# A chunked RWKV-7 recurrence on one core: doubling products over the changed columns only, and next-unit operands made on GpSimd

## The chip, the cores and the metric

One NeuronCore of a Trainium2 chip runs the whole program. The metric is the device time of one execution in microseconds. The engines are TensorE (PE, with its weight loads shown apart as PEld), VectorE (DVE), ScalarE (ACT), GpSimd (POOL) and SyncE (SP, which issues DMAs).

## The reference

Two transformer-like layers on 512 tokens of width 1024. The first has neighbourhood attention beside a gated linear attention, and a convolutional FFN. The second has windowed attention beside a bidirectional RWKV-7 recurrence, a gated merge, an FFN and a per-layer embedding. The change is in the recurrence:

```python
def step(state, inp):                      # rwkv7_bidir_scan, both directions
    r_t, w_t, k_t, v_t, a_t, b_t = inp
    sa = einsum('dbhij,dbhj->dbhi', state, a_t)
    state = state * w_t[..., None, :] + sa[..., :, None] * b_t[..., None, :] + v_t[..., :, None] * k_t[..., None, :]
    y = einsum('dbhij,dbhj->dbhi', state, r_t)
# decay = exp(-exp(-softplus(-w_raw) - 0.5)), a = sigmoid(a0 + al @ a2), kk = k * k_k normalised per head
# k_dir = k * (1 + (a - 1) * k_a); the scan gets (r, decay, k_dir, v, -kk, kk * a)
```

There are 8 heads of 64 and two directions. All matrix work of this stage is fp32.

## The kernel before

The program is a sequence of blocks: mixer, FFN, attention, recurrence, merge and FFN. Every block writes its engine programs out by hand, with counted semaphores. No scheduler moves anything, and each engine works through its own list in order.

The recurrence block (`rwkv_block`) cuts the 512 tokens into 8 chunks of 64 and works in 8 **units**. Unit u is the pair of a head group `fi = u // 2` (two heads, so 128 features on the partitions) and a direction `d = u % 2`. For each unit it does four things.

- It makes the operands. ACT makes `sg` and `rate` by sigmoid (`rates`), DVE a running sum (`sums`: a scan, then one or two tensor operations), and ACT three exponentials (`decays`). DVE then makes `kdir` and a new `rate` (`directed`, three operations) and `bz`, `pc`, `a_s`, `b_s`, `k_s` and `r_s` (`scale`, six operations). PE transposes `a_s`, `b_s`, `k_s` and at times v (`turn`). `turn` and `attention` wait for four counts of `tt_done` per unit.
- It makes five sets of within-chunk products (`attention`, line 2013), which DVE masks.
- It inverts a triangular 64x64 matrix per chunk and head by **doubling** in five rounds, k = 1 to 5 (`double`). Each round is split by head `hh`. PE makes z = ab·x (8 matmuls, two records each), ACT copies z out of PSUM (line 2227), PE makes the products for x and x_t, and DVE writes those entries of x and x_t that the level's mask selects (`copy_predicated`, lines 2368 and 2370). The last round makes x_t alone. At level k only blocks of 2^k columns of one parity change, but all 64 columns are computed and copied.
- It makes the late products (`late`): w and u from x_t (`wr`, 128 columns per matmul), `turn` of the next unit, and then products for the state, the output and the transfer between chunks.

The side work of unit u+1 sits inside the rounds of unit u. On DVE its place is written out by hand:

```python
if k == 1 and u % 2: unit_keys(u // 2 + 1)
elif k == 2:         sums(u + 1)
elif k == 3:         directed(u + 1)
elif k == 4:         scale(u + 1)
```

On ACT, `rates(u + 1)` stands after k = 1 and `decays(u + 1)` after k = 3, each behind the two z copies of its round and each with a load of an activation table. GpSimd has no work in this block. SP loads `lora_g` at the end, behind all of `tt_done`.

After the eight units the block scans over the chunks, normalises and gates.

Of the kernel before, what the change touches and what calls it, by code (L numbers as in the profile page):

```python
# [1877 lines left out]
def rwkv_block(nc, io, C, PV, zr, rw_t):  # L1878
# [6 lines left out]
    with ExitStack() as ctx:  # L1885
# [6 lines left out]
        def column(name, k=0):  # L1892
# [32 lines left out]
                             "ka1_done", "gate_sig"))  # L1925
        levels_loaded, levels_done, masks_loaded, gate_loaded = (
            sem(n) for n in ("levels_loaded", "levels_done", "masks_loaded", "gate_loaded"))
        side_done, side_read, summed, c_done, e_done, kd1, kd_done, tt_done, bonus_done = (
# [8 lines left out]
                             "gstd", "grs", "yn", "yt", "scaled", "gl_done", "with_bonus", "rw_done"))  # L1937

        tiles = lambda a: a.rearrange("p (a b) -> p a b", a=NB)
        tile = lambda a, t: a[:, t * P:t * P + P]  # L1940
# [8 lines left out]
        hp = lambda hh: slice(64 * hh, 64 * hh + 64)  # L1949
        level = lambda side, k: four(levels[:, side, k, :])  # L1950
        R_, K_, V_ = 0, RW_FI, 2 * RW_FI
# [10 lines left out]
        @block.sync  # L1962
        def _(sp):
            sp.dma_start(lora[0:64], io["lora_w"].rearrange("d p n -> p d n")).then_inc(in_loaded, 16)
            sp.dma_start(lora[64:128], io["lora_a"].rearrange("d p n -> p d n")).then_inc(in_loaded, 16)
            at = len(CHUNK_MASKS) * CH
            sp.dma_start(level_in, io["levels"][:, at:]).then_inc(levels_loaded, 16)
            sp.dma_start(masks[:].rearrange("p a b -> p (a b)"), io["levels"][:, 0:at]).then_inc(masks_loaded, 16)
            sp.wait_ge(tt_done, 4 * NU)
            sp.dma_start(lora_g, io["lora_g"]).then_inc(gate_loaded, 16)  # L1970

        @block.tensor
        def _(pe):
# [23 lines left out]

            def attention(u):
                fi, d = unit(u)
                pe.wait_ge(tt_done, 4 * (u + 1))  # L2000
                kinds = ((b_s, a_s, 4, 0), (a_s, b_s, 2, 0), (k_s, r_s, 2, W), (b_s, r_s, 0, 0), (k_s, a_s, 0, W))
# [22 lines left out]
            def double(u, k):  # L2024

                for hh in range(2):
                    if k == 1:
                        pe.wait_ge(a_read, 5 * u + 2)
                    else:
                        pe.wait_ge(cp_done, pr_at(u, k - 1, hh, 1))  # L2030
                        pe.wait_ge(z_read, NZ * u + 2 * (k - 2) + hh + 1)
                    block_products(lambda half, t: bank[hp(half), 4 + hh, t * CH:t * CH + CH],
                                   lambda half, t: ab_t[hp(half), hh, t, :], lambda half, t: x[hp(half), hh, t, :]).then_inc(z_done, 1)
                for hh in range(2):
                    pe.wait_ge(z_read, NZ * u + 2 * (k - 1) + hh + 1)
                    if k < LEVELS - 1:
                        if k == 1:
                            pe.wait_ge(a_read, 5 * u + 3)
                        block_products(lambda half, t: bank[hp(half), 2 + hh, t * CH:t * CH + CH],
                                       lambda half, t: x_t[hp(half), hh, t, :], lambda half, t: z[hp(half), hh, t, :]).then_inc(pr_done, 1)  # L2040
                    if k == 1:
                        pe.wait_ge(a_read, 5 * (u + 1))
                    block_products(lambda half, t: bank[hp(half), hh, t * CH:t * CH + CH],
                                   lambda half, t: z[hp(half), hh, t, :], lambda half, t: x_t[hp(half), hh, t, :]).then_inc(pr_done, 1)

# [113 lines left out]
        def _(act):  # L2159
            def rates(u):  # L2160

                fi, d = unit(u)
                if u:
                    act.wait_ge(tt_done, 4 * u)
                act.wait_ge(side_done, SIDE * u + 1)
# [51 lines left out]
            for u in range(NU):  # L2217
# [33 lines left out]
        def _(dve):  # L2251
            def sums(u):
# [14 lines left out]

            def directed(u):

                fi, d = unit(u)  # L2270
                dve.wait_ge(side_read, SIDE * u + 2)
                dve.wait_ge(kk_done, fi + 1)
                nc.vector.tensor_scalar(kdir[:], rate[:], column("k_a", fi), ka1[:, fi:fi + 1], ALU.mult, ALU.add).then_inc(kd1, 1)
                dve.wait_ge(kd1, u + 1)
                nc.vector.tensor_tensor(kdir[:], kdir[:], zr[:, K_ + fi, :], ALU.mult).then_inc(kd_done, 1)
                nc.vector.tensor_tensor(rate[:], rate[:], rw_t[:, fi, :], ALU.mult).then_inc(kd_done, 1)

            def scale(u):
                fi, d = unit(u)
                dve.wait_ge(e_done, 3 * (u + 1))  # L2280
                dve.wait_ge(kd_done, 2 * (u + 1))
                if u and d == 0:
                    dve.wait_ge(bonus_done, u // 2)
                nc.vector.scalar_tensor_tensor(bz[:, d, :], kdir[:], column("r_k", 4 * d + fi), zr[:, R_ + fi, :], ALU.mult, ALU.mult)
                edge = chunked(e_pos[:])[:, :, CH - 1] if d == 0 else chunked(e_pos[:])[:, :, 0]
                nc.vector.tensor_copy(pc[:, :, 4 * d + fi], edge)
                nc.vector.scalar_tensor_tensor(a_s[:, d, :], rw_t[:, fi, :], -1.0, before[:], ALU.mult, ALU.mult).then_inc(tt_done, 1)
                nc.vector.tensor_tensor(b_s[:, d, :], rate[:], e_neg[:], ALU.mult).then_inc(tt_done, 1)
                nc.vector.tensor_tensor(k_s[:, d, :], kdir[:], e_neg[:], ALU.mult).then_inc(tt_done, 1)
                nc.vector.tensor_tensor(r_s[:, d, :], zr[:, R_ + fi, :], e_pos[:], ALU.mult).then_inc(tt_done, 1)  # L2290

# [30 lines left out]
            def late(u):  # L2322
# [36 lines left out]
            sums(0)  # L2359
            directed(0)  # L2360
            scale(0)
            for u in range(NU):
                attention(u)
                for k in range(1, LEVELS):
                    for hh in range(2):
                        if k < LEVELS - 1:
                            dve.wait_ge(pr_done, pr_at(u, k, hh, 0))
                            nc.vector.copy_predicated(x[:, hh], level(u % 2, k), tiles64(bank[:, 2 + hh, 0:W])).then_inc(cp_done, 1)
                        dve.wait_ge(pr_done, pr_at(u, k, hh, 1))
                        nc.vector.copy_predicated(x_t[:, hh], level(1 - u % 2, k), tiles64(bank[:, hh, 0:W])).then_inc(cp_done, 1)  # L2370
# [12 lines left out]
            dve.wait_ge(rp_read, NU)  # L2383
            for step in range(NCH - 1):
                for d in range(2):
# [425 lines left out]
```

## Time and profile before

| | |
|---|---|
| time, median of 3 runs | 2091.57 us (2091.12 to 2100.21) |
| the profiled execution, its own time | 2093.16 us |
| span in its profile | 2091.4 us, granted TensorE clock 0.936 |
| PE busy | 1807.6 us (86%) |
| DVE busy | 1025.6 us (49%) |
| ACT busy | 729.7 us (35%) |
| POOL busy | 112.9 us (5%) |
| the recurrence block | about 1202 to 1548 us of the span |
| its eight units | from 1227 (first masking) to about 1505 us |

Busy time is what the instructions of an engine cover. For PE it is a poor measure, since matmuls overlap. The granted clock is a share of 2.4 GHz, so 0.5 is 1.2 GHz. In a timeline, several like instructions stand in one row with a count, and the time in brackets is how long the engine idled before it and who ended that.

### The profile page before, as it was taken

The page shows a single profiled execution, that of the slowest core. Times are in us where ns is not written, and L with a number is a line of the kernel's source. Part 1 is how long each engine was busy: PE and PEld are TensorE (multiplying, and loading weights), DVE is VectorE, ACT ScalarE, POOL GpSimd, SP SyncE. Part 2 cuts the span into 40 slices and gives each one's busy share as a digit, 9 for nine tenths or more (in the row PEclk, how much of TensorE's full clock was granted, in tenths as well). Part 3 has the DMA queues.
Part 4 walks back from the last instruction along what each step waited for, and adds up shares of the span by engine and source line. Part 5 has one row for each costly group of instructions (what it writes and reads, how often), then busy time and mean ns, then how long its engine had stood idle before and what let it go on. Part 6 is the DMA issues. An engine that isn't in the chain of part 4 may idle for free. (4 is left out here: it accounts for less than half of the span.)

```text
span 2091.4 us, 37559 instructions
## 1 busy us (share of the span) xinstructions
PE 1807.6 (86%) x16504; PEld 1542.5 (74%) x16504; DVE 1025.6 (49%) x1500; ACT 729.7 (35%) x1193; POOL 112.9 (5%) x133
## 2 busy tenths in 40 slices
PE   6999889838999999639999868888859899999988
PEld 5898768838989989438677657777738688878867
DVE  4145554456534635536454256756565544343445
ACT  3332234414434424223333253434233332232322
POOL 6000000030000000300000000000000200000020
PEclk9999979868999999769999989999979899999999
DMA  5211120102222222022122000000042122222221
GB/s 156 87 55 45 63 81 1 42 17 105 100 87 96 83 98 90 12 96 81 63 89 94 38 23 4 3 4 3 8 171 99 63 101 82 100 101 97 85 81 61
DMA packets 29256, 144.49 MB, mean 69 GB/s; under 512 B 6315, under 2 KB 9659, under 8 KB 14508
## 3 DMA queue, kind: packets, MB, share of 16 engines
q1 hardware_dynamic: 25116, 134.10, 17.9%
q0 software_dynamic: 3696, 7.35, 1.2%
q8 instruction: 126, 2.06, 0.4%
q10 hardware_dynamic: 288, 0.73, 0.1%
q14 instruction: 30, 0.25, 0.0%
HBM read 134.82 MB, written 8.91 MB: 69 GB/s over the span
## 5 line engine op out<-in xcount | busy, mean ns | idle before, releaser
L240 PE MATMUL f_bank<-f_u_hi,f_w_hi 128*128 128x258 f32 x704 | 201.1, 286 | 18.7 <-DVE f_w_lo L228 17.0
L241 PE MATMUL f_bank<-f_u_hi,f_w_lo 128*128 128x258 f32 x704 | 200.7, 285 | 0.0
L242 PE MATMUL f_bank<-f_u_lo,f_w_hi 128*128 128x258 f32 x704 | 199.1, 283 | 0.0
L240 PE MATMUL g_bank<-g_u_hi,g_w_hi 128*128 128x512 f32 x384 | 152.9, 398 | 17.0 <-DVE g_u_lo L2624 13.6
L241 PE MATMUL g_bank<-g_u_hi,g_w_lo 128*128 128x512 f32 x384 | 151.4, 394 | 0.0
L242 PE MATMUL g_bank<-g_u_lo,g_w_hi 128*128 128x512 f32 x384 | 151.2, 394 | 0.0
L240 PE MATMUL g_bank<-g_y_hi,g_w_hi 128*128 128x512 f32 x336 | 133.1, 396 | 18.5 <-DVE g_w_lo L228 11.7
L240 PEld LDWEIGHTS f_bank<-f_u_hi,f_w_hi 128*128 128x128 f32 x704 | 133.4, 190 | 20.3 <-DVE f_w_lo L228 17.8
L215 ACT ACTIVATE g_w_hi<-g_w_raw 128x2048 fp32r<-128x2048 f32 x45 | 85.9, 1909 | 174.4 <-PE g_bank L242 172.0
L242 PEld LDWEIGHTS f_bank<-f_u_lo,f_w_hi 128*128 128x128 f32 x704 | 134.4, 191 | 0.0
L241 PEld LDWEIGHTS f_bank<-f_u_hi,f_w_lo 128*128 128x128 f32 x704 | 133.8, 190 | 0.0
L241 PE MATMUL g_bank<-g_y_hi,g_w_lo 128*128 128x512 f32 x336 | 132.5, 394 | 0.0
L242 PE MATMUL g_bank<-g_y_lo,g_w_hi 128*128 128x512 f32 x336 | 132.3, 394 | 0.0
L228 DVE TENSOR_TENSOR g_w_lo<-g_w_raw,g_w_hi 128x2048 fp32r<-128x2048 f32 x45 | 103.2, 2292 | 48.5 <-ACT g_w_hi L215 48.3
L240 PEld LDWEIGHTS g_bank<-g_u_hi,g_w_hi 128*128 128x128 f32 x384 | 73.0, 190 | 39.5 <-issue 20.0
L228 DVE TENSOR_TENSOR f_w_lo<-f_w_raw,f_w_hi 128x2048 fp32r<-128x2048 f32 x34 | 77.9, 2292 | 47.8 <-ACT f_w_hi L215 47.7
L1606 PE MATMUL a_bank<-a_u_hi,a_w_hi 128*128 128x512 f32 x240 | 98.6, 411 | 1.3 <-ACT a_qkv L1705 0.6
L1610 PE MATMUL a_bank<-a_u_lo,a_w_hi 128*128 128x512 f32 x240 | 98.3, 409 | 0.0
L1608 PE MATMUL a_bank<-a_u_hi,a_w_lo 128*128 128x512 f32 x240 | 98.0, 408 | 0.0
L240 PEld LDWEIGHTS g_bank<-g_y_hi,g_w_hi 128*128 128x128 f32 x336 | 64.1, 191 | 34.6 <-issue 17.0
L242 PEld LDWEIGHTS g_bank<-g_u_lo,g_w_hi 128*128 128x128 f32 x384 | 73.3, 191 | 15.7
L2634 DVE TENSOR_TENSOR h<-g_bank,h 128x512 f32<-128x512 f32 x40 | 27.7, 691 | 114.8 <-PE g_bank L242 114.8
(445 smaller groups left out, 4319.1 us busy)
## 6 DMA issues: line engine op xcount, KB each, us to landing
g_w_raw<-in_w_ff SPq DMA_DIRECT2D x32, 1024.0 KB, 4.8
f_w_raw<-in_w_ffn_in SPq DMA_DIRECT2D x22, 1024.0 KB, 4.8
a_w_raw<-in_w_in SPq DMA_DIRECT2D x18, 1024.0 KB, 4.9
m_w_raw<-in_w_in SPq DMA_DIRECT2D x12, 1024.0 KB, 4.8
f_w_raw<-in_w_ffn_out SPq DMA_DIRECT2D x12, 1024.0 KB, 4.8
m_w_raw<-in_w_o SPq DMA_DIRECT2D x4, 1024.0 KB, 5.1
gate_pre<-rw_t POOLq DMA_DIRECT2D x16, 256.0 KB, 2.3
g_w_raw<-in_w_up SPq DMA_DIRECT2D x4, 1024.0 KB, 8.8
```

Source lines behind the costliest of these rows:

```text
L215: nc.scalar.activation(R.hi[:, r, 0:size], R.raw[:, r, 0:size], ACT.Copy).then_inc(R.hi_done, 1)
L228: nc.vector.tensor_tensor(R.lo[:, r, 0:size], R.raw[:, r, 0:size], R.hi[:, r, 0:size].bitcast(F32), ALU.subtract).then_inc(R.split, 1)
L240: nc.tensor.matmul(out, w_hi, u_hi, start=start, stop=False)
L241: nc.tensor.matmul(out, w_lo, u_hi, start=False, stop=False)
L242: return nc.tensor.matmul(out, w_hi, u_lo, start=False, stop=stop)
L1606: nc.tensor.matmul(tile_bank(g), w_hi, u_hi[:, k, :], start=k == 0, stop=False)
L1608: nc.tensor.matmul(tile_bank(g), w_lo, u_hi[:, k, :], start=False, stop=False)
L1610: last = nc.tensor.matmul(tile_bank(g), w_hi, u_lo[:, k, :], start=False, stop=k == KT - 1)
L2634: nc.vector.tensor_tensor(x[:, t, :], bank[:, (2 * r + m) % 4, :], x[:, t, :], ALU.add).then_inc(R.tile_free, 1)
```

## The change

1. **Doubling.** The moving operand of each doubling matmul is the 32 columns whose parity changes at level k, as a strided view. The result stands packed in PSUM (32 columns per chunk). ACT copies 128 elements per partition and not 256, back into the strided places of `z`. DVE's predicated copies run over 128 and not 256. The weights of each matmul stay 64x64. `z` is cleared once at the start of the block (`z_clear`).
2. **GpSimd.** `directed` (three operations), the copy to `pc`, and `b_s`, `k_s`, `r_s` move to GpSimd, which had no list in this block. DVE keeps `a_s` and `bz` in a new `signed`, after k = 4. `tt_done` now counts 3 per unit, and `sa_done` counts 2. PE's `turn` and `attention`, ACT's `rates` and SP's last load wait for both. DVE's `sums` also waits for `tt_done` of the unit before.

```diff
+        @block.gpsimd
+        def _(pool):
+            def directed(u):
+                fi, d = unit(u)
+                pool.wait_ge(side_read, SIDE * u + 2)
+                if u:
+                    pool.wait_ge(sa_done, 2 * u)
+                pool.wait_ge(kk_done, fi + 1)
+                nc.gpsimd.tensor_scalar(kdir[:], rate[:], column("k_a", fi), ka1[:, fi:fi + 1], ALU.mult, ALU.add).then_inc(kd1, 1)
+                pool.wait_ge(kd1, u + 1)
+                nc.gpsimd.tensor_tensor(kdir[:], kdir[:], zr[:, K_ + fi, :], ALU.mult).then_inc(kd_done, 1)
+                nc.gpsimd.tensor_tensor(rate[:], rate[:], rw_t[:, fi, :], ALU.mult).then_inc(kd_done, 1)
+            def scale(u):
+                pool.wait_ge(e_done, 3 * (u + 1))
+                pool.wait_ge(kd_done, 2 * (u + 1))
...
+                nc.gpsimd.tensor_copy(pc[:, :, 4 * d + fi], edge)
+                nc.gpsimd.tensor_tensor(b_s[:, d, :], rate[:], e_neg[:], ALU.mult).then_inc(tt_done, 1)
+                nc.gpsimd.tensor_tensor(k_s[:, d, :], kdir[:], e_neg[:], ALU.mult).then_inc(tt_done, 1)
+                nc.gpsimd.tensor_tensor(r_s[:, d, :], zr[:, R_ + fi, :], e_pos[:], ALU.mult).then_inc(tt_done, 1)
+            for u in range(NU):
+                directed(u)
+                scale(u)
             def turn(u):
-                pe.wait_ge(tt_done, 4 * (u + 1))
+                pe.wait_ge(tt_done, 3 * (u + 1))
+                pe.wait_ge(sa_done, 2 * (u + 1))
             def double(u, k):
+                compact = lambda b: lambda half, t: bank[hp(half), b, t * CH // 2:t * CH // 2 + CH // 2]
-                    block_products(lambda half, t: bank[hp(half), 4 + hh, t * CH:t * CH + CH],
-                                   lambda half, t: ab_t[hp(half), hh, t, :], lambda half, t: x[hp(half), hh, t, :]).then_inc(z_done, 1)
+                    block_products(compact(4 + hh), lambda half, t: ab_t[hp(half), hh, t, :],
+                                   lambda half, t: parity(x[hp(half), hh, t, :], k, d)).then_inc(z_done, 1)
...
-                        nc.scalar.activation(z[:, hh].rearrange("p a b -> p (a b)"), bank[:, 4 + hh, 0:W], ACT.Copy).then_inc(z_read, 1)
+                        nc.scalar.activation(parities(z[:, hh], k, u % 2), packed(4 + hh, k), ACT.Copy).then_inc(z_read, 1)
...
             def sums(u):
                     dve.wait_ge(e_done, 3 * u)
+                    dve.wait_ge(tt_done, 3 * u)
-            def scale(u):
+            def signed(u):
                 dve.wait_ge(e_done, 3 * (u + 1))
+                nc.vector.scalar_tensor_tensor(a_s[:, d, :], rw_t[:, fi, :], -1.0, before[:], ALU.mult, ALU.mult).then_inc(sa_done, 1)
                 if u and d == 0:
                     dve.wait_ge(bonus_done, u // 2)
+                dve.wait_ge(kd_done, 2 * (u + 1))
+                nc.vector.scalar_tensor_tensor(bz[:, d, :], kdir[:], column("r_k", 4 * d + fi), zr[:, R_ + fi, :], ALU.mult, ALU.mult).then_inc(sa_done, 1)
...
+            nc.vector.memset(z[:], 0.0).then_inc(z_clear, 1)
...
-                            nc.vector.copy_predicated(x[:, hh], level(u % 2, k), tiles64(bank[:, 2 + hh, 0:W])).then_inc(cp_done, 1)
+                            nc.vector.copy_predicated(parities(x[:, hh], k, u % 2), level(u % 2, k), packed(2 + hh, k)).then_inc(cp_done, 1)
...
-                        elif k == 3:
-                            directed(u + 1)
                         elif k == 4:
-                            scale(u + 1)
+                            signed(u + 1)
```

The order of instructions shows the two places that matter. The first is VectorE in the rounds k = 3 to 5 of the unit that starts at 1262.80 us. Before:

```order
L2370 COPY_PREDICATED r_x_t<-r_levels,r_bank 128x256
L2273 TENSOR_SCALAR r_kdir<-r_rate,params,r_ka 128x512
L2275 TENSOR_TENSOR r_kdir<-r_kdir,zr 128x512
L2276 TENSOR_TENSOR r_rate<-r_rate,rw_t 128x512
L2368 COPY_PREDICATED r_x<-r_levels,r_bank 128x256
```

```order
L2284 SCALAR_TENSOR_TENSOR r_bz<-r_kdir,params,zr 128x512
L2286 COPY r_pc<-r_cum 128x8
L2287 SCALAR_TENSOR_TENSOR r_a_s<-rw_t,r_before 128x512
L2288 TENSOR_TENSOR r_b_s<-r_rate,r_e_neg 128x512
L2289 TENSOR_TENSOR r_k_s<-r_kdir,r_e_neg 128x512
L2290 TENSOR_TENSOR r_r_s<-zr,r_cum 128x512
L2370 COPY_PREDICATED r_x_t<-r_levels,r_bank 128x256 x2
```

The same place now, from the second sum of the next unit on:

```order
L2305 TENSOR_TENSOR r_before<-r_cum,r_sg 128x512
L2397 COPY_PREDICATED r_x<-r_levels,r_bank 128x16x8
L2399 COPY_PREDICATED r_x_t<-r_levels,r_bank 128x16x8
L2397 COPY_PREDICATED r_x<-r_levels,r_bank 128x16x8
L2399 COPY_PREDICATED r_x_t<-r_levels,r_bank 128x16x8
L2397 COPY_PREDICATED r_x<-r_levels,r_bank 128x8x16
L2399 COPY_PREDICATED r_x_t<-r_levels,r_bank 128x8x16
L2397 COPY_PREDICATED r_x<-r_levels,r_bank 128x8x16
L2399 COPY_PREDICATED r_x_t<-r_levels,r_bank 128x8x16
L2315 SCALAR_TENSOR_TENSOR r_a_s<-rw_t,r_before 128x512
L2319 SCALAR_TENSOR_TENSOR r_bz<-r_kdir,params,zr 128x512
L2399 COPY_PREDICATED r_x_t<-r_levels,r_bank 128x4x32 x2
```

Seven of nine side operations have left VectorE's list between round 3 and the last copies. The second place is GpSimd from the start of the block, where before there was nothing. Now:

```order
L1990 ISA
L1990 TENSOR_SCALAR r_kdir<-r_rate,params,r_ka 128x512
L1992 TENSOR_TENSOR r_kdir<-r_kdir,zr 128x512
L1993 TENSOR_TENSOR r_rate<-r_rate,rw_t 128x512
L2000 COPY r_pc<-r_cum 128x8
L2001 TENSOR_TENSOR r_b_s<-r_rate,r_e_neg 128x512
L2002 TENSOR_TENSOR r_k_s<-r_kdir,r_e_neg 128x512
L2003 TENSOR_TENSOR r_r_s<-zr,r_cum 128x512
```

The seven operations behind the ISA row come eight times, once per unit, and the ISA row comes once. TensorE's list keeps its order and its counts of matmuls. Only the doubling products read 64x32 where they read 64x64.

## Rows read from the trace of the kernel before

**Rows 1.** Stretches, two units: us; busy us (records) PE, PEld, DVE, ACT, POOL; clock; DMA.

```profile
1262.80:1297.50 34.70, 29.25 (x900) 25.52 (x893) 24.23 (x41) 14.49 (x27) 0.00 (x0) 1.00 0.02 4
...
1334.00:1369.80 35.80, 30.61 (x900) 26.91 (x893) 24.17 (x42) 14.49 (x27) 0.00 (x0) 0.95 0.01 3
```

**Rows 2.** Timeline, one doubling round: start, us, engine, line, operation, tiles, count, [idle<-releaser].

```profile
1274.23 0.63 PE L2021 MATMUL r_bank<-r_x_t,r_z 64*64 64x64 f32 x16
...
1274.70 0.63 PE L2021 MATMUL r_bank<-r_z,r_x_t 64*64 64x64 f32 x16
...
1276.31 0.38 ACT L2227 ACTIVATE r_z<-r_bank 128x256 f32<-128x256 f32 x1 [2.38 <-PE r_bank L2021]
```

**Rows 3.** Groups by form: busy us, mean ns of one, then idle before.

```profile
L2227 ACT ACTIVATE r_z<-r_bank 128x256 f32<-128x256 f32 x80 | 29.4, 382 | 70.8 <-PE r_bank L2021 70.0
...
L2198 ACT ACTIVATE r_wu<-r_bank 128x512 f32<-128x512 f32 x16 | 9.6, 598 | 31.6 <-PE r_bank L2021 31.6
...
L2370 DVE COPY_PREDICATED r_x_t<-r_levels,r_bank 128x256 f32<-128x256 uint8 x80 | 34.5, 441 | 3.9 <-PE r_bank L2021 2.8
...
L2307 DVE COPY_PREDICATED r_x_t<-r_levels,r_bank 128x512 f32<-128x512 uint8 x8 | 5.7, 714 | 0.0
```

**Rows 4.** Groups by form, weight loads of 64 and of 16 columns.

```profile
L2021 PEld LDWEIGHTS r_bank<-r_x_t,r_z 64*64 64x64 f32 x1280 | 44.3, 135 | 1.9 <-ACT r_z L2227 1.2 <-issue 0.4
...
L720 PEld LDWEIGHTS m_bank<-m_proj 64*16 64x16 f32 x16 | 0.3, 90 | 0.1
```

**Rows 5.** Timeline, 32 product records spread over four corners of the array.

```profile
1262.30 0.65 PE L2013 MATMUL r_bank<-r_r_s,r_k_s 64*64 64x64 f32 x32
```

**Rows 6.** Timeline, end of the doubling of the unit from 1262.80.

```profile
1283.23 0.74 DVE L2284 SCALAR_TENSOR_TENSOR r_bz<-r_kdir,params,zr 128x512 f32<-128x512 f32 x1
...
1283.90 1.33 PE L2021 MATMUL r_bank<-r_x_t,r_z 64*64 64x64 f32 x32
...
1286.38 0.77 DVE L2370 COPY_PREDICATED r_x_t<-r_levels,r_bank 128x256 f32<-128x256 uint8 x2
```

**Rows 7.** GpSimd and VectorE together in the FFN: timeline, then GpSimd's additions (min/median/max ns).

```profile
881.96 0.68 DVE L1478 TENSOR_TENSOR h<-h,f_acc 128x512 f32<-128x512 f32 x1
882.12 3.15 POOL L310 TENSOR_TENSOR f_a<-f_a,f_c 128x512 f32<-128x512 f32 x2 [1.29 <-ACT f_c L320]
...
882.56 1.75 DVE L1475 SCALAR_TENSOR_TENSOR f_acc<-f_acc,params,f_c 128x512 f32<-128x512 f32 x1
...
L310 POOL TENSOR_TENSOR g_sq_sum<-g_sq_sum,g_branch x14: 1262/1292/2883, 1617.7 to 2017.2; 128x512 f32<-128x512 f32 x14
```

**Rows 8.** Timeline, side work for the next unit in the rounds of rows 2.

```profile
1272.71 0.68 ACT L2168 ACTIVATE r_rate<-r_bank,params 128x512 f32<-128x512 f32 x1
...
1276.28 1.23 DVE L2258 TENSOR_TENSOR_SCAN r_cum<-r_reset,r_sg 128x512 f32<-128x512 f32 x1
...
1278.77 0.63 ACT L2172 ACTIVATE r_e_neg<-r_cum 128x512 f32<-128x512 f32 x1
...
1279.82 0.61 ACT L2174 ACTIVATE r_before<-r_before 128x512 f32<-128x512 f32 x1
```

**Rows 9.** Timeline, the first unit's last operand and what waited for it.

```profile
1221.38 0.68 DVE L2290 TENSOR_TENSOR r_r_s<-zr,r_cum 128x512 f32<-128x512 f32 x1
...
1222.12 1.12 PE L1991 MATMUL r_bank<-consts,r_a_s 128*128 128x128 f32 x4 [11.62 <-DVE r_r_s L2290]
```

**Rows 10.** Stretches before and in a fall of the clock (columns as in rows 1).

```profile
1351.40:1354.80 3.40, 3.07 (x98) 2.94 (x99) 3.08 (x8) 0.86 (x3) 0.00 (x0) 1.00 0.02 5
1354.80:1358.20 3.40, 1.67 (x45) 1.42 (x43) 3.23 (x8) 0.38 (x1) 0.00 (x0) 1.00 0.02 5
1358.30:1361.60 3.30, 3.30 (x31) 2.97 (x28) 0.00 (x0) 1.01 (x2) 0.00 (x0) 0.50 0.00 0
```

**Rows 11.** Timeline, the products behind the doubling, unit from 1262.80 and unit from 1334.00.

```profile
1286.95 1.96 PE L2021 MATMUL r_bank<-r_wr,r_x_t 64*64 64x128 f32 x32 [1.72 <-DVE r_x_t L2370]
...
1357.84 3.30 PE L2021 MATMUL r_bank<-r_wr,r_x_t 64*64 64x128 f32 x32 [1.72 <-DVE r_x_t L2370]
```

More of the change, by code:

```diff
@@ L1925, in rwkv_block @@
                              "ka1_done", "gate_sig"))
-        levels_loaded, levels_done, masks_loaded, gate_loaded = (
-            sem(n) for n in ("levels_loaded", "levels_done", "masks_loaded", "gate_loaded"))
+        levels_loaded, levels_done, masks_loaded, gate_loaded, z_clear = (
+            sem(n) for n in ("levels_loaded", "levels_done", "masks_loaded", "gate_loaded", "z_clear"))
         side_done, side_read, summed, c_done, e_done, kd1, kd_done, tt_done, bonus_done = (
@@ L1949, in rwkv_block, with level @@
         hp = lambda hh: slice(64 * hh, 64 * hh + 64)
-        level = lambda side, k: four(levels[:, side, k, :])
+        HALF_W = NB * CH // 2
+        parity = lambda a, k, par: a.rearrange("p (n s b) -> p n s b", s=2, b=1 << k)[:, :, par, :]
+        parities = lambda a, k, par: a.rearrange("p t (n s b) -> p t n s b", s=2, b=1 << k)[:, :, :, par, :]
+        packed = lambda b, k: bank[:, b, 0:HALF_W].rearrange("p (t n b) -> p t n b", t=NB, b=1 << k)
+        def level(side, k):
+            return parity(levels[:, side, k, :], k, side).unsqueeze(1).broadcast_to([P, NB, CH >> (k + 1), 1 << k])
         R_, K_, V_ = 0, RW_FI, 2 * RW_FI
@@ L1968, in _ @@
             sp.dma_start(masks[:].rearrange("p a b -> p (a b)"), io["levels"][:, 0:at]).then_inc(masks_loaded, 16)
-            sp.wait_ge(tt_done, 4 * NU)
+            sp.wait_ge(tt_done, 3 * NU)
+            sp.wait_ge(sa_done, 2 * NU)
             sp.dma_start(lora_g, io["lora_g"]).then_inc(gate_loaded, 16)
+        @block.gpsimd
[11 more added lines that the diff above has]
+            def scale(u):
+                fi, d = unit(u)
+                pool.wait_ge(e_done, 3 * (u + 1))
+                pool.wait_ge(kd_done, 2 * (u + 1))
+                edge = chunked(e_pos[:])[:, :, CH - 1] if d == 0 else chunked(e_pos[:])[:, :, 0]
+                nc.gpsimd.tensor_copy(pc[:, :, 4 * d + fi], edge)
[5 more added lines that the diff above has]
+                scale(u)
         @block.tensor
@@ L2038, in double @@
                             pe.wait_ge(a_read, 5 * u + 3)
-                        block_products(lambda half, t: bank[hp(half), 2 + hh, t * CH:t * CH + CH],
-                                       lambda half, t: x_t[hp(half), hh, t, :], lambda half, t: z[hp(half), hh, t, :]).then_inc(pr_done, 1)
+                        block_products(compact(2 + hh), lambda half, t: x_t[hp(half), hh, t, :],
+                                       lambda half, t: parity(z[hp(half), hh, t, :], k, d)).then_inc(pr_done, 1)
                     if k == 1:
                         pe.wait_ge(a_read, 5 * (u + 1))
-                    block_products(lambda half, t: bank[hp(half), hh, t * CH:t * CH + CH],
-                                   lambda half, t: z[hp(half), hh, t, :], lambda half, t: x_t[hp(half), hh, t, :]).then_inc(pr_done, 1)
+                    block_products(compact(hh), lambda half, t: z[hp(half), hh, t, :],
+                                   lambda half, t: parity(x_t[hp(half), hh, t, :], k, 1 - d)).then_inc(pr_done, 1)
             def keys_values(u):
@@ L2163, in rates @@
                 if u:
-                    act.wait_ge(tt_done, 4 * u)
+                    act.wait_ge(tt_done, 3 * u)
+                    act.wait_ge(sa_done, 2 * u)
                 act.wait_ge(side_done, SIDE * u + 1)
@@ L2266, in sums @@
                     nc.vector.tensor_tensor(cum[:], before[:], sg[:], ALU.add).then_inc(c_done, 1)
[L2268 to L2276, printed above, removed]
-            def scale(u):
+            def signed(u):
                 fi, d = unit(u)
                 dve.wait_ge(e_done, 3 * (u + 1))
-                dve.wait_ge(kd_done, 2 * (u + 1))
+                nc.vector.scalar_tensor_tensor(a_s[:, d, :], rw_t[:, fi, :], -1.0, before[:], ALU.mult, ALU.mult).then_inc(sa_done, 1)
                 if u and d == 0:
                     dve.wait_ge(bonus_done, u // 2)
[L2284 to L2290, printed above, removed]
+                dve.wait_ge(kd_done, 2 * (u + 1))
+                nc.vector.scalar_tensor_tensor(bz[:, d, :], kdir[:], column("r_k", 4 * d + fi), zr[:, R_ + fi, :], ALU.mult, ALU.mult).then_inc(sa_done, 1)
             def bonus(u):
@@ L2359, in _ @@
             sums(0)
-            directed(0)
-            scale(0)
+            signed(0)
             for u in range(NU):
@@ L2367, in _ @@
                             dve.wait_ge(pr_done, pr_at(u, k, hh, 0))
-                            nc.vector.copy_predicated(x[:, hh], level(u % 2, k), tiles64(bank[:, 2 + hh, 0:W])).then_inc(cp_done, 1)
+                            nc.vector.copy_predicated(parities(x[:, hh], k, u % 2), level(u % 2, k), packed(2 + hh, k)).then_inc(cp_done, 1)
                         dve.wait_ge(pr_done, pr_at(u, k, hh, 1))
-                        nc.vector.copy_predicated(x_t[:, hh], level(1 - u % 2, k), tiles64(bank[:, hh, 0:W])).then_inc(cp_done, 1)
+                        nc.vector.copy_predicated(parities(x_t[:, hh], k, 1 - u % 2), level(1 - u % 2, k), packed(hh, k)).then_inc(cp_done, 1)
                     if u + 1 < NU:
```

7 lines of the change are left out of this document (6 added, 1 removed).

## The prediction

> **What bounds the kernel now.** The page comes first. It gives 86% busy to PE, but the recurrence is only some 280 of 2091 us, and what the change is worth must be read there. The stretches of two whole units [rows 1] show that no engine is full: in 34.70 us PE covers 29.25, DVE 24.23, ACT 14.49 and GpSimd nothing. A unit is a chain that goes round PE, ACT and DVE. The timeline of one round shows its links [rows 2]: 16 product records, the next 16 begin 0.47 us later, and a z copy follows on ACT. At its other end each round waits for DVE's predicated copies. The list of VectorE places side work between these copies, and the timeline of the unit's end shows what that does [rows 6]: PE's last 32 records are over at 1285.23, but six side operations hold DVE from 1283.23 to 1286.38, the two x_t copies end at 1287.15, and PE stood idle 1.72 us for them [rows 11].
>
> All times below are per unit of about 35 us. Seven of the eight units prepare a next one.
>
> **Step A: shorter copies.** ACT's z copy takes 382 ns for 256 elements and 598 for 512 [rows 3], so 0.84 ns each. At 128 it should take 275, or 0.11 less. DVE's predicated copy takes 441 and 714 ns [rows 3], 1.07 ns each, so about 305, or 0.14 less. Strided places may cost some of this. A round's critical path meets either the z copy of the first head or the x_t copy of the second, and not both. I take 0.13 us a round: 5 rounds x 8 units x 0.13 = **-5.2 us**. The one clearing of `z` (512 elements) runs while DVE waits at the block's start and costs nothing.
>
> **Step B: the products themselves.** The rows of before hold no 32-column product. In a doubling group, records follow each other every 29 ns (0.47 us for 16) on two corners of the array, so 58 ns per corner. That is the time in which 64 columns stream, but each corner also loads 64 weight columns per record. A load lasts 135 ns for 64 columns and 90 for 16 [rows 4]: 45 ns more for 48 columns, so the columns of a 64-wide load take some 60 ns. The change halves the streaming and leaves the load. One bound is therefore no gain. The other is half the spacing: the queue itself is able to do that, since with four corners 32 records took 0.65 us [rows 5], or 14 ns apart. I take no gain in spacing, because the load's own columns are as long as the whole spacing, and nothing in a row says that a corner can load faster.
>
> The Trainium skill says more than that in "TensorEngine Tiling (Array Packing)", section Instruction Overhead: about 60 cycles per matmul, so that one column costs as much as 60. By that rule step B is nothing whatever the loads do. The trace disagrees with the rule as a floor, since 14 ns is about 34 cycles of 2.4 GHz [rows 5], so I leave the gain a chance.
>
> **Step C: six operations leave DVE, and two stay.** `directed` after k = 3 ran under ACT's three exponentials, which end at 1280.43 [rows 8] and hold the next z copies, so its time on DVE was covered. `scale` was not covered. Without any side work the x_t copies could end at 1285.7 in place of 1287.15: 1.4 us. What is late next is PE's own last group. But `a_s` and `bz` read two SBUF tensors each, and so do GpSimd's operations, which then run at the same time. The FFN stage shows that pair [rows 7]: a DVE operation of 0.68 or 0.75 us alone takes 1.75 beside two GpSimd additions, and these take 3.15 for two where the median of one is 1.29. I price it as taking turns. GpSimd starts its last three at about 1280.7 and runs until about 1285.3, DVE reaches `a_s` at 1283.0, waits up to 1 us, and is through with `bz` near 1285.9. Then the copies end at 1286.5. That leaves 0.6 of the 1.4: 7 x 0.6 = **-4.2 us**. The bounds are 0 and -10.
>
> **Step D: the same turns earlier.** GpSimd can start `directed` once the second sigmoid is done, at 1273.39 [rows 8], and needs about 0.9 + 1.29 + 1.29 with small gaps, so until 1277.2. DVE's scan, also with two SBUF inputs, starts at 1276.28. It would wait until GpSimd's third operation ends, up to 1 us. The exponentials wait for the sum. They started at 1278.77, just behind it and behind a table load, so most of the delay comes through: 0.7 x 7 = **+4.9 us**, with 0 and 9 as bounds. The Trainium skill ("SBUF — State Buffer", section SBUF: two separate sides) calls the shared pair an exclusive lock for the whole instruction, and it agrees with rows 7 in kind. Taken literally it makes C 0 and D +9, and the sum 8 us more. DVE's copies from PSUM have one SBUF input, the mask, and by that page do not take part. No row here pairs them with GpSimd.
>
> **Step E: the first unit.** No doubling covers its operands: PE waits until `r_s` ends at 1222.06 [rows 9]. On DVE the six operations of `scale` take 3.15 us, as in a later unit [rows 6]. On GpSimd it is a small copy and three of 1.3 to 1.6 us, about 5, and `directed` ends about 1 us later. That is **+3 us**, between 1 and 5. In later units, the last operand is made at about 1285.3, and PE asks for it behind the `wr` products, from 1288.9 [rows 11]. That is 3 us of cover. If it is gone, every further microsecond counts seven times. DVE's new wait in `sums` is for work long done by then. SP's last load still has the whole scan over the chunks for cover. GpSimd's one ISA row stands ahead of its first wait, in a time in which that engine had nothing.
>
> **Step F: the clock.** The granted clock was 1.00 in most of this stage. In one place it fell to 0.50 [rows 10]. The stretch before had 45 product records of 64 columns; a normal doubling stretch has 98. The same products behind the doubling took 1.96 us at 2.4 GHz and 3.30 at 1.2 GHz [rows 11]. After the change the doubling has about as many records, but of 32 columns. If streaming is what keeps the clock up, every doubling stretch looks like one of 49, so like the one before the fall. I expect a fall in the doubling of most units. The doubling itself loses little, for 32 columns at 1.2 GHz take as long as 64 did and the load is no faster anyway. The `wr` products pay: 1.34 x 8 = **+10.7 us**. The bounds are 0 and +20, the latter when the low level reaches on into the transposes and the lora products.
>
> **The sum.** -5.2 - 4.2 + 4.9 + 3.0 + 10.7 = +9.2 us. Against the profiled execution's own 2093.16 us that is 2102.4. The median of the runs shown is 1.6 lower, so the forecast is **2101 us**, own range 2094 to 2109. The stated limit of 0.5%, about what a measurement of this kernel can tell from no change, is 10.5 us.
>
> **The rivals.**
>
> 1. *The clock stays up*, because weight loads or the mere number of records count. For it: the fall was in a stretch in which PE was also idle. Against it: the count of rows 10. Without F the sum is -1.5, so 2090 us.
> 2. *The spacing does halve*, because loads overlap better than I think. Each round then sheds 96 x 14 ns = 1.35 us of PE's list. In rounds 2 to 4 ACT's sigmoids and exponentials and DVE's sums would then set much of the pace, so I count two rounds in full: 1.35 x 2 x 8 = -22 us. With the rest of the sum it is 2079, and 2068 if the clock stays up too. For it: rows 5. Against it: rows 4.
> 3. *GpSimd and DVE hardly disturb each other here*, because the turns fall luckily. C becomes -10, D 0, E +1, and with the clock term the sum is about -3.5, so 2088; without it 2077.
> 4. *Slower: a second low stretch per unit.* The low level begins by round 2 or 3 of the doubling and lasts through the transposes and the first late products. A second pass over 1.3 to 2 us of PE work at half rate adds 8 x 1.5 = 12 us: 2113. It decides from the point at which the low clock covers more than the `wr` products. For it: a unit with one fall at the end took 35.80 against 34.70 us [rows 1], and here the fall would come earlier. Against it: after 3.3 us of `wr` products the level rose again [rows 10].
>
> **How the numbers follow.** Forecast 0.42, rival 1 0.17, rival 2 0.19, rival 3 0.09, rival 4 0.13. Slower than 2102.0 are rival 4 and 0.45 of the forecast: 0.13 + 0.19 = 0.32. Faster than 2081.1 are two thirds of rival 2 (0.13), half of rival 3 (0.05) and the lower end of rival 1 (0.04): 0.22. The rest, 0.46, is within 0.5%. The range from 2072 to 2112 leaves out the lower part of rival 2 and the upper half of rival 4.
>
> **What would show it.** B: groups of 16 records still begin 0.47 us apart, and a 32-column record is some 25 ns shorter. A: z copies near 275 ns and predicated copies near 305. C and D: `a_s`, `bz` and the scan with means well above 0.75 and 1.23 us, and GpSimd's additions above 1.3. E: the first transposes about 3 us later. F: granted clock below 0.8 in stretches inside the units, and the `wr` products near 3.3 us in most. The forecast is wrong if the clock holds 1.00 through the units, or if groups of 16 begin 0.3 us apart or less.

## The result, and the profile after

The changed kernel takes 2126.18 us (median of 4 runs, 2121.73 to 2129.53) against 2095.49 us of the kernel before beside it (4 runs, 2091.12 to 2100.21). The ratio is **1.0145**, with a 95% interval from 1.0109 to 1.0180: slower by some 31 us, and outside the predicted range. The profiled execution took 2124.47 us, its span 2122.6. Ratios leave out a run over 1.5% above the fastest of its kernel as a slow one; that was so once, for a run of 2165.19 us of e4, which the medians still count.

Stretches come first, as in [rows 1]. The first fence is the kernel before: its first seven units, from the first masking of unit 0 to that of unit 7. The second is the changed kernel: the same seven units, then a whole unit, then two stretches inside that unit's doubling, one just before the clock falls and one just after. Columns as in [rows 1].

```profile
1227.30:1476.50 249.20, 210.77 (x6170) 181.69 (x6165) 155.45 (x283) 102.29 (x189) 0.00 (x0) 0.99 0.02 4
```

```profile
1230.30:1508.90 278.60, 257.05 (x6195) 233.35 (x6189) 123.79 (x234) 96.35 (x190) 49.88 (x49) 0.77 0.02 4
...
1352.46:1390.83 38.37, 35.78 (x900) 32.87 (x892) 19.94 (x35) 13.70 (x27) 7.12 (x7) 0.78 0.01 3
...
1362.00:1365.40 3.40, 2.33 (x80) 2.33 (x80) 2.15 (x7) 1.19 (x4) 2.04 (x3) 1.00 0.02 5
1365.60:1368.90 3.30, 3.30 (x64) 3.30 (x66) 3.20 (x4) 2.27 (x4) 1.02 (x1) 0.50 0.00 0
1365.60:1382.50 16.90, 16.90 (x275) 16.57 (x276) 6.83 (x14) 5.68 (x12) 4.89 (x5) 0.50 0.01 2
```

The seven units have grown from 249.2 to 278.6 us: 29.4 of the 31.2 us by which the span is longer. DVE's busy time fell by 32 us and ACT's by 6, as the change wants, and PE's rose by 46 although it was given less to stream. The column of the granted clock points to the reason: 0.99 before, 0.77 now. In the unit shown the level is 0.50 for 17 us, from round 3 of the doubling to the end of the `wr` products, and in all of it PE's records, whose ends are modelled, leave no gap (16.90 of 16.90). Ahead of the fall, PE had waits at the full clock (2.33 of 3.40 us busy). There 64 records fill 3.3 us, 52 ns each; before, 98 records were done in 3.4 us at the full clock [rows 10].

The timeline shows the same pace in single groups. All are groups of 16 records of 32 columns, first at clock 1.00, then at 0.50. Columns as in [rows 2]. The last two rows are the `wr` products of this unit and the first unit's first transposes, which answer to [rows 11] and [rows 9].

```profile
1363.56 0.63 PE L2060 MATMUL r_bank<-r_x_t,r_z 64*64 64x32 f32 x16
...
1364.03 0.63 PE L2060 MATMUL r_bank<-r_z,r_x_t 64*64 64x32 f32 x16
...
1367.25 1.04 PE L2060 MATMUL r_bank<-r_x_t,r_z 64*64 64x32 f32 x16
...
1368.11 1.04 PE L2060 MATMUL r_bank<-r_z,r_x_t 64*64 64x32 f32 x16
...
1378.35 3.66 PE L2060 MATMUL r_bank<-r_wr,r_x_t 64*64 64x128 f32 x32
...
1224.81 1.11 PE L2029 MATMUL r_bank<-consts,r_a_s 128*128 128x128 f32 x4 [13.91 <-POOL r_r_s L2003]
```

At the full clock a group starts 0.47 us after the one ahead, exactly as the 64-column groups of [rows 2]: halving the streamed columns gained nothing. At the low clock it is 0.86 us (1367.25 to 1368.11).

The groups by form show what got longer. They are from 1227 to 1500 us; each row gives the busy time and mean of one, then the idle time before.

```profile
L2060 PEld LDWEIGHTS r_bank<-r_x_t,r_z 64*64 64x64 f32 x1120 | 58.4, 194 | 2.2 <-issue 1.5 <-DVE r_ak_t L2333 0.5
...
L2270 ACT ACTIVATE r_z<-r_bank 128x128 f32<-128x128 f32 x70 | 18.9, 281 | 90.4 <-PE r_bank L2060 90.4
...
L2399 DVE COPY_PREDICATED r_x_t<-r_levels,r_bank 128x128 f32<-128x128 uint8 x70 | 22.8, 325 | 31.5 <-PE r_bank L2060 31.4
...
L2302 DVE TENSOR_TENSOR_SCAN r_cum<-r_reset,r_sg 128x512 f32<-128x512 f32 x7 | 11.9, 1697 | 0.0
...
L2319 DVE SCALAR_TENSOR_TENSOR r_bz<-r_kdir,params,zr 128x512 f32<-128x512 f32 x7 | 5.2, 744 | 0.0
```

The weight load of 64 columns, 135 ns in [rows 4], now averages 194 over stretches at both levels; within the low one of the unit shown it takes 223. ACT and DVE wait for PE: DVE's idle time before the `x_t` copies is 31.5 us, where [rows 3] had 3.9. The copies themselves are shorter, as forecast. The scan, on the other hand, takes 1697 ns, where it took 1230 alone [rows 8].

### The profile page after: what moved, and what is told of

Its sections match the earlier page's. It is cut to its first block and busy times, and to the rows that moved or that the text cites. A ratio compares the mean times of both kernels' runs of the same rounds, so it can differ in the third digit from the quotient of the medians.

```text
span 2122.6 us, 37584 instructions
## 1 busy us (share of the span) xinstructions
PE 1854.2 (87%) x16504; PEld 1594.4 (75%) x16504; DVE 989.1 (47%) x1445; ACT 724.3 (34%) x1193; POOL 172.1 (8%) x189
## 5 line engine op out<-in xcount | busy, mean ns | idle before, releaser
L240 PEld LDWEIGHTS g_bank<-g_u_hi,g_w_hi 128*128 128x128 f32 x384 | 73.0, 190 | 39.8 <-issue 20.0
L241 PEld LDWEIGHTS g_bank<-g_u_hi,g_w_lo 128*128 128x128 f32 x384 | 73.4, 191 | 14.1
```

Source lines behind the costliest of these rows:

```text
L240: nc.tensor.matmul(out, w_hi, u_hi, start=start, stop=False)
L241: nc.tensor.matmul(out, w_lo, u_hi, start=False, stop=False)
```

## The experiments

Theory T: the clock falls because the doubling streams half the columns, and at the low level weight loads and products both go slower. Rivals: the loss comes from GpSimd's operations and their turns with VectorE (G, later C), or from reading the streamed operand in pieces (S). Expectations stand as they were written before each run. Ratios are against the kernel before on the same chip.

| run | us, median | ratio, 95% interval | seven units, us | clock there |
|---|---|---|---|---|
| changed kernel | 2126.18 | 1.0145, 1.0109 to 1.0180 | 278.6 | 0.77 |
| e1 GpSimd part alone | 2092.13 | 0.9977, 0.9968 to 0.9987 | 244.7 | 1.00 |
| e2 narrow doubling alone | 2148.73 | 1.0254, 1.0237 to 1.0271 | 296.4 | 0.72 |
| e3 changed, 64-column products | 2089.11 | 0.9976, 0.9958 to 0.9994 | 240.4 | 1.00 |
| e4 changed, unused products added | 2141.64 | 1.0152, 1.0069 to 1.0234 | 292.3 | 0.85 |
| e5 changed, first 32 columns | 2140.34 | 1.0223, 1.0189 to 1.0258 | 287.3 | 0.74 |
| e6 only z products narrow | 2090.86 | 0.9986, 0.9971 to 1.0001 | 245.8 | 0.96 |
| e7 = e3, first unit on VectorE | 2086.75 | 0.9966, 0.9953 to 0.9980 | 244.0 | 1.00 |
| e8 = e7, two moves | 2075.08 | 0.9913, 0.9880 to 0.9947 | 231.3 | 1.00 |
| e9 = e8, 32-column products | 2137.20 | 1.0209, 1.0173 to 1.0244 | 286.8 | 0.75 |
| e10 = e8, whole copies | 2081.22 | 0.9941, 0.9922 to 0.9960 | 239.4 | 1.00 |

The last two columns come from each profiled execution. The medians of the kernel before were 2096.25 beside e1 to e4, 2093.82 beside e5 to e8, 2095.53 beside e9 and e10.

### The two halves apart: e1 and e2

e1 keeps the GpSimd part and takes the doubling of before back:

```
-  block_products(compact(4 + hh), ..., parity(x[...], k, d))
+  block_products(bank[hp(half), 4 + hh, t * CH:t * CH + CH], ..., x[...])
-  activation(parities(z[:, hh], k, u % 2), packed(4 + hh, k), Copy)
+  activation(z[:, hh], bank[:, 4 + hh, 0:W], Copy)
   (x and x_t products and predicated copies likewise)
```

> The change's GpSimd half alone: GpSimd makes the directed keys, chunk decays and scaled operands, the doubling keeps 64 streamed columns and whole copies. Theory T (the loss is the clock, which falls because the doubling's products stream half the columns): granted clock 1.00 through the units, unit period near the 34.7 us of before, time 2088 to 2101 us (scale off VectorE -4, scan disturbed +5, first unit +3 around the 2095 of before). Rival G (the loss is GpSimd's slower operands and its taking turns with VectorE): 2115 us or more, clock at 1.00.

e2 is the other half: the products and copies of the change, with `directed` and `scale` on VectorE as before and no GpSimd program.

> The change's doubling half alone: products stream the 32 changed columns into packed PSUM and the copies are narrow, VectorE makes all keys and operands as before. T: granted clock 0.50 through most of the doubling of every unit, 32-column records 50 ns or so apart there, 2115 to 2135 us. G: no loss, the shorter copies alone count, 2085 to 2092 us.

e1: 2092.13 us, within T's numbers, and a little faster than before. e2: 2148.73 us, slower than T's upper end and slower than the whole change. So the loss is all in the doubling, and G falls. That e2 is worse than both halves together was not foreseen. Its clock is 0.72 where the changed kernel has 0.77, and its VectorE has the seven operations back; which of these costs the 22 us was not settled.

The seven units of e1, then of e2:

```profile
1229.90:1474.60 244.70, 207.65 (x6198) 179.10 (x6193) 143.43 (x234) 102.61 (x190) 50.01 (x49) 1.00 0.02 4
...
1227.70:1524.10 296.40, 272.55 (x6225) 247.64 (x6221) 144.99 (x283) 96.13 (x189) 0.00 (x0) 0.72 0.01 4
```

In e2 PE is busy 272.55 us, 62 more than before, for the same number of records (within 1%).

### The streamed columns alone: e3, e9 and e6

e3 changes only what PE streams. The copies stay narrow and pick their 32 columns out of 64 in PSUM:

```
-  compact = lambda b: lambda half, t: bank[hp(half), b, t * CH // 2:t * CH // 2 + CH // 2]
+  compact = lambda b: lambda half, t: bank[hp(half), b, t * CH:t * CH + CH]
-  parity(x[hp(half), hh, t, :], k, d)
+  x[hp(half), hh, t, :]
-  packed(4 + hh, k)
+  picked(4 + hh, k, u % 2)
   (z and x_t likewise)
```

> The changed kernel, but the doubling's products stream all 64 columns again; ScalarE and VectorE still copy only the 32 changed columns, now picked out of the 64 in PSUM; GpSimd part kept. T: TensorE's work is that of before and the clock stays at 1.00, copies 0.1 us shorter: 2082 to 2098 us, 28 to 44 us under the changed kernel. G: about the changed kernel's 2126 us.

2089.11 us: 37 us less, by streaming twice as much. Seven units of e3 and two neighbouring groups at the full clock:

```profile
1230.30:1470.70 240.40, 204.74 (x6165) 178.17 (x6159) 130.78 (x234) 94.56 (x189) 53.11 (x49) 1.00 0.02 4
```

```profile
1312.49 0.63 PE L2060 MATMUL r_bank<-r_x_t,r_z 64*64 64x64 f32 x16
...
1312.96 0.63 PE L2060 MATMUL r_bank<-r_z,r_x_t 64*64 64x64 f32 x16
```

With 64 columns the groups stand 0.47 us apart, just as the 32-column groups of the changed kernel do at clock 1.00. PE busy is 204.74 us against 257.05.

e9 makes the same step in the other direction, from the fastest version (e8, below), with narrow products put back.

> e8 with the changed kernel's narrow products again (32 streamed columns, packed PSUM), all else as e8: the other way round from e3. T: low clock in every unit again, 2105 to 2125 us, 30 to 50 us over e8 although TensorE is asked for less. Rival C (the loss of the changed kernel was contention, which e8 removed): 2068 to 2080 us.

The seven units of e8, then of e9:

```profile
1226.30:1457.60 231.30, 205.46 (x6213) 179.52 (x6212) 121.42 (x235) 94.56 (x189) 53.44 (x49) 1.00 0.02 5
```

```profile
1226.00:1512.80 286.80, 262.97 (x6184) 240.16 (x6187) 127.48 (x235) 96.11 (x189) 53.38 (x49) 0.75 0.02 4
```

2137.20 us, 62 us over e8, at clock 0.75 against 1.00. Rival C falls. T's direction holds, but its number (up to 2125) was too low: at the low clock e8's better order brought nothing, and the kernel was 11 us slower than the changed one. The slower doubling had also shifted the meetings: the moved `bz` took 1671 ns in e9, where it had taken 744 in the changed kernel. A unit takes 39.8 us in the changed kernel, 41.0 in e9 and 42.3 in e2 (the stretches divided by 7), and it is low for a larger part of the last two. What sets where in a unit the level falls and rises was not settled by these runs. Nor do they separate the two things that e3 and e9 change together, the streamed width and the packing of the result in PSUM.

e6 is a dose between: only the z products are narrow.

```
   block_products(compact(4 + hh), ..., parity(x[hp(half), hh, t, :], k, d))
-  block_products(compact(2 + hh), ..., parity(z[hp(half), hh, t, :], k, d))
+  block_products(whole(2 + hh), ..., z[hp(half), hh, t, :])
   (x_t likewise)
```

> A dose between the two: only the z products (a third of the doubling's products) stream 32 columns, the x and x_t products stream 64 again, all copies narrow, GpSimd part kept. T with a gate that falls by degrees of streaming: clock mostly 1.00, 2086 to 2098 us, little above e3's 2089; if the clock needs all of the streaming that before had: low stretches in every unit, 2100 to 2120 us. Rival S: 2089 plus a third of the 37 us between e3 and the changed kernel, 2101 us, with no change of the clock.

2090.86 us at clock 0.96: a third of the halving costs 2 to 4 us over e3 (by the medians, and by each median against its own kernel before), where a third of 37 is 12, so the loss is not in proportion to the number of narrow products. Two whole units, one of 34.50 and one of 36.80 us:

```profile
1262.40:1296.90 34.50, 29.94 (x897) 26.87 (x892) 19.84 (x35) 13.45 (x27) 7.59 (x7) 0.95 0.01 4
1366.00:1402.80 36.80, 32.33 (x898) 28.52 (x892) 16.85 (x33) 13.56 (x27) 7.14 (x7) 0.91 0.01 3
```

### Is the narrow product slow by itself? e4 and e5

e4 leaves the narrow products as they are and adds work to PE in places where it waits:

```
+  def filler(b):
+      nc.tensor.matmul(bank[:, b, W:W + 256], C("ident"), masks[...][:, 0:256], start=True, stop=True)
   (z products of both heads)
+  if k > 1: filler(3)
   (x and x_t products of both heads)
+  if k < LEVELS - 1: filler(5)
```

> The changed kernel with one unused product of 128 x 256 (0.43 us at the full clock) added after the z products of rounds 2 to 5 and after the last product of rounds 1 to 4, where TensorE waits for a copy: 64 in all, up to 27 us of added TensorE time. T: the granted clock stays at 1.00 in most of the doubling and the time falls although work is added, to 2090 to 2112 us. Rival S (strided or packed 32-column products or their loads are slow by themselves, and the clock is only a symptom): 2126 us or up to 27 us more, 2126 to 2153 us.

The median, 2141.64 us, missed T's 2090 to 2112, and by this number alone S would stand. The runs spread from 2111.83 to 2165.19 us, though, and the stretches of the profiled one show two kinds of units. The first row is a whole unit, the second lies within a unit of 50.9 us:

```profile
1230.30:1267.20 36.90, 34.47 (x893) 27.82 (x881) 16.79 (x33) 13.78 (x27) 7.13 (x7) 1.00 0.01 3
1348.30:1385.60 37.30, 37.30 (x449) 29.68 (x447) 12.50 (x24) 8.69 (x17) 7.12 (x7) 0.50 0.01 2
```

The first unit kept the clock and took 36.90 us with narrow products and eight added ones. The same unit took 39.7 in the changed kernel, without them, and 34.9 in e3. The 2.0 us over e3 are less than the added work: an added product stands 0.63 us before what follows it (0.43 had been expected), so eight are 5.0 if none were hidden. So narrow products at the full clock are not slow, and S falls for the units that kept it. In the units that fell, the level stayed at 0.50 for 37 us, and the added work was paid at double price. Unused work was thus a poor remedy: of these seven units it kept two at 1.00 and three at 0.91 to 0.96, and two fell to 0.63 and 0.64 and took over 50 us each.

e5 streams 32 columns that lie side by side. It leaves out the right columns, and computes with the first 32 instead; the amount of work is unchanged.

```
-  parity(x[hp(half), hh, t, :], k, d)
+  x[hp(half), hh, t, 0:CH // 2]
   (z and x_t likewise)
```

> The changed kernel, but each product streams the first 32 columns, side by side, instead of the 32 changed ones picked in blocks of 1 << k (this leaves the right columns out of the computation; the amount of work is the same). T (the clock falls because the streamed columns are halved, whichever they are): 2120 to 2135 us, clock at 0.50 through most of the doubling. Rival S (the strided read of the streamed operand slows the products): under 2105 us.

2140.34 us at clock 0.74, 5 over T's band and 35 over S's. The pieces in which the operand is read are not the cause. That e5 is 14 us slower than the changed kernel is unexplained.

### What the other steps are worth at the full clock: e7, e8, e10

The clock had hidden the rest of the change. In e3 it can be seen. Two groups of VectorE from 1227 to 1500 us, then a timeline of one unit's side work:

```profile
L2302 DVE TENSOR_TENSOR_SCAN r_cum<-r_reset,r_sg 128x512 f32<-128x512 f32 x7 | 14.6, 2090 | 0.0
L2319 DVE SCALAR_TENSOR_TENSOR r_bz<-r_kdir,params,zr 128x512 f32<-128x512 f32 x7 | 12.3, 1753 | 0.0
```

```profile
1310.99 1.27 POOL L1993 TENSOR_TENSOR r_rate<-r_rate,rw_t 128x512 f32<-128x512 f32 x1
...
1311.37 1.98 DVE L2302 TENSOR_TENSOR_SCAN r_cum<-r_reset,r_sg 128x512 f32<-128x512 f32 x1
...
1317.93 1.27 POOL L2002 TENSOR_TENSOR r_k_s<-r_kdir,r_e_neg 128x512 f32<-128x512 f32 x1
...
1318.37 0.30 DVE L2397 COPY_PREDICATED r_x<-r_levels,r_bank 128x128 f32<-128x128 uint8 x1 [0.16 <-PE r_bank L2060]
...
1319.05 0.71 DVE L2315 SCALAR_TENSOR_TENSOR r_a_s<-rw_t,r_before 128x512 f32<-128x512 f32 x1
1319.16 1.72 POOL L2003 TENSOR_TENSOR r_r_s<-zr,r_cum 128x512 f32<-128x512 f32 x1
...
1319.68 1.75 DVE L2319 SCALAR_TENSOR_TENSOR r_bz<-r_kdir,params,zr 128x512 f32<-128x512 f32 x1
```

Whoever starts second waits: `r_s` takes 1.72 us, 0.45 over its undisturbed 1.27, since `a_s` started 0.11 earlier; then `bz`, 0.74 alone, is not through until 0.55 us after `r_s` ends at 1320.88. (Spans on GpSimd are rough, so these sums hold to a tenth or two.) The predicated copy, with one input from SBUF and one from PSUM, takes 0.30 us beside GpSimd's `k_s`; the mean of the `x_t` copies is 323 ns in e3 and 327 in e2, where GpSimd does nothing. The Trainium skill ("SBUF — State Buffer", section SBUF: two separate sides) describes an exclusive lock between a VectorE operation with two SBUF inputs and GpSimd, held for the whole operation, and the traces agree with it in each of these rows, but for some 0.2 us by which `bz` ends sooner than a start after `r_s` would give.

e7 puts the first unit's operands back on VectorE (`for u in range(1, NU)` on GpSimd; `first()`, with the operations of before, on VectorE).

> e3 (64-column products, narrow copies, GpSimd part) with the first unit's directed keys, edge and scaled operands on VectorE as before. Step E (first unit +3 us): 2.6 us under e3, about 2086.5 us, and the first masking 3 us earlier. Rival: the first unit's operands are off the path that ends last, no difference from e3.

2086.75 us, 2.4 under e3. Against the kernel before on its own chip each stands at 0.9966 and 0.9976, with overlapping intervals, so the times show no more than consistency. The traces are sharper: from the start of the block's first reciprocal to the first transposes it is 11.65 us in the kernel before and 11.70 in e7, and 13.94 in e3. The step is worth 2.2 to 2.3 us. The seven units, for which the two kernels have the same code, still took 244.0 and 240.4 us, so differences of 3 or 4 us between single traces mean little.

e8 then moves two things:

```
 GpSimd, directed(u):
+    pool.wait_ge(c_done, u + 1)
     tensor_tensor(rate, rate, rw_t, mult)
 VectorE:
+    elif k == 3: gated(u + 1)      # bz, was the end of signed
     elif k == 4: signed(u + 1)     # a_s
```

> e7 with two moves against the contention that e3 shows (scan 2.09 us against 1.22, bz 1.75 against 0.74): bz is made after round 3 instead of after round 4, when GpSimd is idle, and GpSimd's product of rates and keys waits for VectorE's sums. Step D (GpSimd disturbs VectorE, and VectorE's side work is on the path): scan and bz return to 1.2 and 0.75 us, 0.8 to 1.7 us less per unit, 6 to 13 us in all, 2074 to 2081 us. Rival (the side work is hidden behind TensorE): within 2 us of e7.

2075.08 us, inside what was expected and 11.7 under e7: the fastest of all, 0.9% faster than before and 2.4% faster than the changed kernel (2126.18). The groups of e8, from 1221 to 1500 us:

```profile
L2303 DVE TENSOR_TENSOR_SCAN r_cum<-r_reset,r_sg 128x512 f32<-128x512 f32 x7 | 8.5, 1217 | 0.0
L2323 DVE SCALAR_TENSOR_TENSOR r_bz<-r_kdir,params,zr 128x512 f32<-128x512 f32 x7 | 7.5, 1066 | 0.0
```

The scan is back at 1217 ns. `bz` fell to 1066 and not to 750, for it now meets the moved product of rates and keys. It starts 0.35 us before that ends at 1341.74 (e8's timelines of GpSimd and of VectorE):

```profile
1340.47 1.27 POOL L1994 TENSOR_TENSOR r_rate<-r_rate,rw_t 128x512 f32<-128x512 f32 x1 [1.99 <-DVE r_before L2306]
...
1341.39 0.90 DVE L2323 SCALAR_TENSOR_TENSOR r_bz<-r_kdir,params,zr 128x512 f32<-128x512 f32 x1
```

e10 takes e8 and copies whole (the copies of before: 64 columns, no `parities`).

> e8 with whole copies of 64 columns in place of the picked 32, all else as e8. Step A (copies 0.1 us shorter, worth 5.2 us where the doubling waits for them): e8 plus 5 us, 2080 us; if the copies are hidden behind TensorE: 2075 us as e8.

2081.22 us: the shorter copies are worth 6.1 us by the medians and 4.4 when each is set against the kernel before on its own chip. No run of e10 is as fast as the slowest of e8, but the intervals of the two ratios overlap slightly.

## Why the prediction was wrong, step by step

The prediction gave 2101 us, with 2072 to 2112 as its range, and 0.32 to slower. The time was 2126.

**Step F failed, in its size.** That the clock would fall in the doubling of most units was right: 0.77 over seven units, with each of them between 0.68 and 0.79, and the `wr` products at 3.66 us. The error is in one clause: "The doubling itself loses little, for 32 columns at 1.2 GHz take as long as 64 did and the load is no faster anyway." Step B had just argued that the weight load sets the pace, and F then left that pace the same at half the clock. It does not stay: the groups stand 0.86 us apart, not 0.47, a corner gets a record every 107 ns where it was 58, so 1.8 times as long, and a load takes 223 ns in the low stretch where it was 135. So the term of +10.7 us, bounded by +20, is **+37 us** by e3 against the changed kernel and +62 by e9 against e8. Per unit the changed kernel takes 39.8 us (278.6 / 7) and e3 34.3: 5.5 us, of which at most 1.7 are the `wr` products (3.66 against 1.96 [rows 11]) and nearly 4 is left for the rest, above all the doubling that was to lose little. In the units looked at, z of round 3 to the `wr` products is 13.39 us in the changed kernel (1364.96 to 1378.35) and 10.85 in e3 (1310.94 to 1321.79), though e3 has waits in it. No row of before shows a group of narrow or 64-column products at the low clock (the records of [rows 10] and [rows 11] at 0.50 stream 128 columns), so the term needed two bounds, a load of constant duration and one that grows with the clock's period. The second was left out. Why the pace follows the clock, by the load or by another cost of each product, stays open.

**Step A** was right: 281 and 325 ns where 275 and 305 were forecast, and for the -5.2 some 3 to 6 us at the full clock (4.4 or 6.1 by e10 over e8; 3.0 between e1 and e3, whose intervals overlap). In the low stretches of the changed kernel it can save nothing, since PE's records leave no gap there.

**Step B** was right for the full clock: 0.47 us between groups with 32 and with 64 columns. The Trainium skill's section Instruction Overhead ("TensorEngine Tiling (Array Packing)"), by which a narrow product costs as much as one of some 60 columns, comes to the same result here; no run separates it from the load. The prediction held 14 ns, 34 cycles, against that rule. But the kernel issues one matmul for every two records, so the same row is 28 ns, some 67 cycles, a matmul, and does not contradict it if matmuls are what is counted.

**Steps C and D**: the mechanism was right, and its traces are in e3, but it was not at work where the forecast put it. At the low clock `bz` took 744 ns, undisturbed, for GpSimd was through by the time the slowed doubling let VectorE reach it; the scan still grew, to 1697. At the full clock C, D and E together are -4.1 us (e1 against 2096.25; its interval allows some 3 to 7), where +3.7 was forecast. With +2.3 for E, and the scan's 0.66 us (1877 ns in e1 against 1218 in e2) seven times over as D, +4.6 if all of it is on the path, C comes to -11, at or past its bound of -10. Part of that may be clock: two of the seven units of before hold a fall (0.95 each, one of them in [rows 1]), none of e1's does (1.00), and at the 1.34 us of [rows 11] that is up to 2.7 us. Another part may be what `directed` took off VectorE, which step C held to be covered. This is worked out, not shown by a run. In its count step C was one short: seven operations leave VectorE, not six.

**Step E** was right within its bounds: the first transposes began at 1224.81 and not at 1222.12. Counted from the block's first reciprocal, it is 2.3 us of these 2.7 (13.95 against 11.65), and e7 takes them back.

**The rivals.** Rival 1 (the clock stays up) fell; its 2090 is almost the time of e3, the kernel in which the clock does stay up, with the full width streamed. Rival 2 (half the spacing) fell with step B. Rival 3 fell: the two engines disturb each other in e3 as forecast. Rival 4 had the right sign, and "by round 2 or 3" for the fall was right as well, but it added a second stretch at 1.5 us a unit, at 2113, and not the price of the first.

Step by step from kernel to kernel, by medians: 2096.25, -4.1 (e1), -3.0 (e3's shorter copies), +37.1 (narrow streaming) give the changed kernel's 2126. Of these the second lies within the spread of the runs. And the terms depend on their order: without the GpSimd part the change to the doubling costs 52 us (e2).

## What to carry to other kernels

Where small products follow each other no faster with fewer streamed columns (0.47 us a group here, with 64 and with 32), streaming fewer saves no time and may lose the clock. A pace that did not depend on the columns can still depend on the clock: price a fall over everything that TensorE does in it. Keep the full products and narrow only what other engines copy. When GpSimd takes work from VectorE, place its two-input operations against VectorE's so that they do not meet. Here that was worth more (11.7 us) than moving the work itself (4.1), at the full clock only.

## What was not expected of the hardware

- More work for TensorE made the kernel faster. e3 streams twice the columns of the changed kernel in the doubling and is 37 us faster; e8 and e9 show it again with 62 us.
- The clock did not rise for mere busyness, as far as records with modelled ends show it. In the changed kernel PE was busy for 16.90 of 16.90 us at 0.50, and in e4 for 37.30 of 37.30, at 449 records.
- Narrow copies from PSUM cost the same packed (325 ns, changed kernel) as picked out of 64 columns in blocks of 1 << k. The group of e3:

```profile
L2399 DVE COPY_PREDICATED r_x_t<-r_levels,r_bank 128x128 f32<-128x128 uint8 x80 | 25.2, 323 | 9.9 <-PE r_bank L2060 9.5
```
